# Attention inside a stream of projections: the last three value blocks of a head pair move into the next pair's first turn

## The reference, cut to what matters

```python
h = _rmsnorm(x, norm_g)
a_val, a_glu, z_a, q, k, v, z_b, g_logits = split(h @ w_in)
y_a = (_conv_module(a_val, a_glu, ...) * silu(z_a)) @ w_pw_a      # 31 taps along the tokens, per channel
attn = _neighbourhood_attention(q, k, v, rpb)                     # 16 heads of 64, window of 8 x 16 tokens
y_b = (attn * silu(z_b)) @ w_o_b
y = x + (sigmoid(g_a) * y_a + sigmoid(g_b) * y_b) @ w_out         # then a last rmsnorm
# attention of one query block j of 16 columns, against a band of 32 key columns:
s = einsum('bjqhd,bijkhd->bjqhik', qb, k_band) * scale + bias     # outside the window: -1e30
p = softmax(s)
o = einsum('bjqhik,bijkhd->bjqhd', p, v_band)
```

## Time and profile before

| | |
|---|---|
| median of three runs | 1718.92 us (1718.72 to 1720.77) |
| the profiled execution | 1718.98 us, span 1717.2 us |
| granted TensorE clock | 0.999 of full |
| PE busy | 1706.2 us, 99% |
| DVE, ACT, POOL busy | 1174.1, 470.5, 201.9 us |
| one unit of the loop | 145.02 us |
| the last unit and what follows it, 1198.93 to 1314.00 us | DVE 92.8 of 115.07 us, PE 113.4 |

### The profile page before, as it was taken

How to read it: one execution, slowest core, us unless ns; L and a number is a source line. 1 busy time by engine, 2 the same in 40 slices (tenths; PEclk the granted TensorE clock), 3 DMA queues, 4 the chain that set the end, 5 groups by cost and what they waited for, 6 DMA issues and landing times.

```text
span 1717.2 us, 25052 instructions
## 1 busy us (share of the span) xinstructions
PE 1706.2 (99%) x8644; PEld 1407.6 (82%) x8644; DVE 1174.1 (68%) x1875; ACT 470.5 (27%) x931; POOL 201.9 (12%) x251
## 2 busy tenths in 40 slices
PE   9999999999999999999999999999999999999998
PEld 7888888888888888888888888888887888888887
DVE  6549256896798589679678958967996755335332
ACT  5321123223122222222222222231234244003222
POOL 1110011001011001101101100010110064000001
PEclk9999999999999999999999999999999999999999
DMA  8761345445535444634552554454558775643223
GB/s 308 228 104 48 97 132 149 132 124 150 138 92 167 127 111 128 162 101 134 154 147 71 149 154 111 124 153 121 135 164 307 233 222 162 199 130 109 74 92 129
DMA packets 299204, 247.79 MB, mean 144 GB/s; under 512 B 117815, under 2 KB 252999, under 8 KB 298988
## 3 DMA queue, kind: packets, MB, share of 16 engines
q1 hardware_dynamic: 246666, 153.04, 32.5%
q10 hardware_dynamic: 48578, 79.97, 14.3%
q0 software_dynamic: 3872, 13.75, 3.1%
HBM read 158.78 MB, written 87.90 MB: 144 GB/s over the span
## 4 chain that ended last, share of the span: by engine, by line
PE 91%; DMA 4%; DVE 3%; issue 1%; SPq 1%; ACT 1%; POOL 0%; ACTq 0%; DVEq 0%; POOLq 0%
PE pg L1631 72%; PE pg L1649 11%; PE pS L1789 2%; PE pS L1808 2%; DMA x_d<-work 1%; PE pO L1808 1%; PE pO L1789 1%; DMA p_d<-work 1%; DVE xs L1188 1%; SPq L507 0%; DVE work L1385 0%; DMA work<-p_d 0%; DVE work L1387 0%; SPq L571 0%; PE pg L1676 0%
## 5 line engine op out<-in xcount | busy, mean ns | idle before, releaser
L1631 PE MATMUL pg<-xs,ws 128*128 128x512 f32 x5688 | 1304.2, 390 | 0.8 <-issue 0.6
L1631 PEld LDWEIGHTS pg<-xs,ws 128*128 128x128 f32 x5688 | 1064.2, 188 | 230.0 <-issue 8.2
L1302 DVE SCALAR_TENSOR_TENSOR work<-work 128x1551 f32<-128x1551 f32 x240 | 439.0, 1829 | 16.5 <-issue 11.8
L1649 PE MATMUL pg<-ws,xs 128*128 128x512 f32 x942 | 218.6, 389 | 0.7 <-DVE xs L1235 0.7
L1649 PEld LDWEIGHTS pg<-ws,xs 128*128 128x128 f32 x942 | 176.5, 188 | 37.9 <-issue 1.3
L733 POOL TENSOR_TENSOR work<-work 128x384 f32<-128x384 bf16 (+1 forms) x72 | 62.5, 868 | 964.2 <-DVE small L1375 952.1
L1026 ACT ACTIVATE work<-work,small 128x384 f32<-128x384 f32 (+1 forms) x192 | 109.4, 571 | 207.8 <-DVE small L1375 207.6
L1180 DVE TENSOR_TENSOR ws<-raw,ws 128x1024 fp32r<-128x1024 f32 x88 | 109.1, 1240 | 55.6 <-ACT ws L786 55.6
L786 ACT ACTIVATE ws<-raw 128x1024 fp32r<-128x1024 f32 x89 | 93.8, 1055 | 133.9 <-PE pg L1631 99.1
L1375 DVE CUSTOM_DVE_ANT_0 work<-pS,work 128x384 f32<-128x384 f32 (+1 forms) x128 | 58.0, 504 | 86.1 <-PE pS L1789 85.2
L1387 DVE STREAM_TRANSPOSE work<-work 128x384 f32<-128x384 f32 (+1 forms) x192 | 102.6, 534 | 6.6
(11 more groups left out here) (142 smaller groups left out, 1027.1 us busy)
## 6 DMA issues: line engine op xcount, KB each, us to landing
raw<-in_w_in SPq DMA_DIRECT2D x70, 512.0 KB, 3.8
p_d<-work SPq DMA_DIRECT2D x256, 96.0 KB, 2.1
work<-p_d ACTq DMA_DIRECT2D x63, 384.0 KB, 3.7
work<-v_d SPq DMA_DIRECT2D x128, 96.0 KB, 2.7
p_d<-work SPq DMA_DIRECT2D x128, 64.0 KB, 1.9
work<-p_d ACTq DMA_DIRECT2D x32, 256.0 KB, 3.0
v_d<-work ACTq DMA_DIRECT2D x24, 256.0 KB, 2.2
za_d<-work ACTq DMA_DIRECT2D x24, 256.0 KB, 2.1
```

Source lines behind the costliest of these rows:

```text
L1302: nc.vector.scalar_tensor_tensor(cv[:, 0:CLEN], u[:, k:k + CLEN], cur[:, k:k + 1], cv[:, 0:CLEN], ALU.mult, ALU.add).then_inc(tap_ok, 1)
L1631: last = nc.tensor.matmul(pg[b][:], wt(s, wpart)[:, k * P:(k + 1) * P], xs[:, k, xpart, chunk(n)], start=(j == 0 and wpart == 1), stop=(j ...
L1649: last = nc.tensor.matmul(pg[b][:], xs[:, k, xpart, t * P:(t + 1) * P], wt(s0 + k // 2, wpart)[:, chunk(k % 2)], start=(k == 0 and xpart = ...
```

## The change

The values of visit 3 of a pair (blocks 9, 10, 11) leave slot 41 and stand at slot 1 of the next unit, right ahead of that unit's first scores. In the code they are visit -1 of the next unit, with counts -3 to -1. `take_o` of these blocks moves on DVE from slot 42 to slot 2 of the next unit, behind the probabilities of block 1. In the last unit visit 3 stays at slot 30, and pair 6's last values come in at slot 1.

The values now need the pair's V until slot 1 of the next unit, so `load_v` moves on SP from the end of a unit to slot 4 of the next, right ahead of the first two blocks' stores. Its wait is taken by a separate nop, so that the 16 transfers are issued one after another behind it. The last third of `tb` is ready later, so the store of `tb` is split: two thirds at slot 33 (`tb_out`), the last third at slot 3 of the next unit (`tb_late`).

```diff
-VALUE_SLOTS = (11, 21, 31, 41)
+VALUE_SLOTS = (1, 11, 21, 31)
-FIRST_VALUES = (8, 15, 22, 29)
+FIRST_VALUES = (None, 8, 15, 22)
-LAST_VALUES = (8, 16, 23, 30)
+LAST_VALUES = (1, 8, 16, 23, 30)
@@ values_at
-    return table.index(slot) if slot in table else None
+    return table.index(slot) - 1 if slot in table else None
@@ load_v
-                after(sp, pv_done, used)
+                if not isinstance(i, int):
+                    sp.wait_ge(pv_done, used)
+                    sp.nop(nofuse=True)
+                else:
+                    after(sp, pv_done, used)
@@ SyncE, unit
                     c = scores_at(i, slot - 3)
+                    if c == 0 and not tiles is FIRST_UNIT:
+                        load_v(i, BLOCKS * i)
                     if c is not None:
                         for b in blocks_of(c)[0:2]:
                             store_probs(i, b)
...
-                if not last:
-                    load_v(i + 1, BLOCKS * i + BLOCKS)
@@ ScalarE, unit
-                    if values_at(i, slot - 2) == VISITS - 1 and not last:
-                        act.wait_ge(o_out, BLOCKS * i + BLOCKS)
-                        act.dma_start(row_of(tb_d, i), tb).then_inc(tb_out, 16)
+                    if values_at(i, slot - 2) == VISITS - 2 and not last:
+                        act.wait_ge(o_out, BLOCKS * i + 2 * BLOCKS // NCH)
+                        act.dma_start(row_of(tb_d, i)[:, 0:2 * CH], tb[:, 0:2 * CH]).then_inc(tb_out, 16)
+                    if slot == 3 and not first:
+                        act.wait_ge(o_out, BLOCKS * i)
+                        act.dma_start(row_of(tb_d, i - 1)[:, 2 * CH:TOK], tb[:, 2 * CH:TOK]).then_inc(tb_late, 16)
@@ VectorE, take_o
+                def take_o(count):
+                    b = count % BLOCKS
+                    dve.wait_ge(pv_done, BLOCKS * i + (count + 1))
+                    if count // VISIT < VISITS - 1:
+                        dve.wait_ge(qk_done, blk(i, blocks_of(count // VISIT + 1)[2], 1))
+                    if count >= 0:
+                        bz, _, oz = grp(i, s)
+                        dve.wait_ge(g_out[bz], oz)
@@ VectorE, evac of z_b
-                        after(dve, tb_out, 16 * i)
+                        after(dve, tb_late if n == NCH - 1 else tb_out, 16 * i)
@@ TensorE, values
-                def values(b):
+                def values(count):
+                    b = count % BLOCKS
-                    pe.wait_ge(p_in[b % VISIT], 16 * VISITS * i + 16 * (b // VISIT) + 16)
+                    pe.wait_ge(p_in[b % VISIT], 16 * VISITS * i + 16 * (count // VISIT) + 16)
```

More of the change, by code:

```diff
@@ L337, in build @@
         st_out = [sem(f"st_out{i}") for i in range(3)]
-        tb_out, c_out = sem("tb_out"), sem("c_out")
+        tb_out, tb_late, c_out = sem("tb_out"), sem("tb_late"), sem("c_out")
         cur_ok, curg_ok = sem("cur_ok"), sem("curg_ok")
@@ L578, in load_tb_early @@
                 sp.wait_ge(tb_out, 16 * (PAIRS - 1))
+                sp.wait_ge(tb_late, 16 * (PAIRS - 1))
                 piece_y(S_YB + 1)
@@ L1387, in probs @@
                     nc.vector.transpose(t, t).then_inc(tr_done, 1)
-                def take_o(b):
+                def take_o(count):
+                    b = count % BLOCKS
                     s, j = seg_of(b)
-                    dve.wait_ge(pv_done, BLOCKS * i + (b + 1))
-                    if b // VISIT < VISITS - 1:
-                        dve.wait_ge(qk_done, blk(i, blocks_of(b // VISIT + 1)[2], 1))
-                    bz, _, oz = grp(i, s)
-                    dve.wait_ge(g_out[bz], oz)
+                    dve.wait_ge(pv_done, BLOCKS * i + (count + 1))
[4 more added lines that the diff above has]
+                        dve.wait_ge(g_out[bz], oz)
                     z = tb[:, chunk(s)].rearrange("p (r j c) -> p j r c", j=4, c=QB)[:, j]
@@ L1781, in scores @@
                         after(pe, t_ok, 24 * i + 2 * b)
-                        after(pe, o_out, BLOCKS * i + max(b - VISIT, 0))
+                        after(pe, o_out, BLOCKS * i + (b - VISIT))
                     for qpart, kpart in ((q_lo, k_hi), (q_hi, k_lo), (q_hi, k_hi)):
@@ L1799, in values @@
                     if b % VISIT == 0:
-                        after(pe, t_ok, 24 * i + 2 * (b + VISIT))
-                        after(pe, o_out, BLOCKS * i + max(b - VISIT, 0))
+                        after(pe, t_ok, 24 * i + 2 * (count + VISIT))
+                        after(pe, o_out, BLOCKS * i + (count - VISIT))
                     for n, (c, a, z) in enumerate(REACH[s]):
@@ L1805, in values @@
                             rows = slice(HD * h, HD * h + HD)
-                            p = pt_of(i, b)[:, h].rearrange("p (a c q) -> p c a q", a=4, q=32)
+                            p = pt_of(None if count < 0 else i, b)[:, h].rearrange("p (a c q) -> p c a q", a=4, q=32)
                             o = o_of(b)[rows, :].rearrange("p (a q) -> p a q", a=4)
```

## The result

The changed kernel takes 1723.26 us (median of nine runs, 1721.08 to 1726.68), the kernel before 1719.42 beside it (nine runs, 1718.72 to 1721.39): ratio 1.0020, 95% interval 1.0010 to 1.0029. By the ratio it is slower by 3.4 us, between 1.7 and 5.0; the two medians are 3.8 us apart. That is just the 0.2% which the prediction took for what a measurement of this kernel can tell from no change. The forecast was 1721.2 in a range of 1717.5 to 1726.5. In two later jobs the medians stood 2.1 and 2.3 us apart, and the interval of the second (0.9999 to 1.0017) does not exclude no change.

The account below looks back on a forecast made before the run. The prediction took TensorE, at its own pace without idle time in the loop, as the bound. Interruptions saved (-1.54), loop (0) and last unit (+3.8) gave +2.3 us on 1718.98, hence 1721.2 us, range 1717.5 to 1726.5.

Parts of the forecast that it names:

- The gain of 1.54: TensorE, pairs 0 to 6: one interruption of a matmul run fewer per pair, 0.22 us each, 1.54 us gained.
- SP and the third block: V's issues delay stores; DVE starts the third block 14.9 us (loop) or 14.6 (last unit) after t, TensorE's slot 1.
- the rival without late stores: V's issues as short as its data, stores not held up: 0.3 us lost in the last unit, 1717.7; chance 0.08.
- DVE's own arrival: Loop: with three take_o ahead, DVE reaches the third block at 12.75 us, then stands still until 14.9.
- No pause in the loop: Loop, slot 8: group 2 released at 22.15 us, TensorE asks at 22.3; fits by 0.15 us, costs nothing.
- The first rival: Loop units pause too, once the third block starts after 15.1 us; 1724.6 with stores 0.6 us later; chance 0.33.
- The last unit: New TensorE pause of 3.2 us at slot 6, waiting for group 1; DVE's chain stays 5.6 us late.
- the term of 3.8: Last unit: its end moves 5.6 us, 1.8 of it moved values, so 3.8 us lost (ends 3.4 and 6.5).
- The clock rival: Granted clock falls to 1.2 GHz during the last unit's 3.2 us pause: 1.6 us more, 1722.8; chance 0.04.
- Against: 1.00 throughout: Argument against the clock falling: the granted clock read 1.00 in both profiled windows of the kernel before.
- The sum: Whole kernel: -1.54 + 0 + 3.8 = +2.3 us, hence 1721.2 us.
- 1719.8 to 1722.3: Whole-kernel time if the last unit loses and the loop does not: the main forecast, chance 0.52.

Follow-up runs that it names:

- v_split: Changed kernel with V's 16 transfers in units 1 to 7 issued half by SyncE, half by GpSimd; ratio 0.9997 to the kernel before.
- v_pool: Changed kernel with V of units 1 to 7 issued by GpSimd, ahead of its third bias kind; ratio 1.0053 to the kernel before.
- v_dose: Changed kernel with two more 96 KB transfers issued by SyncE behind V's 16 in each loop unit; ratio 1.0039 to the kernel before.
- v_alone: Kernel before with only V's transfers moved ahead of the first stores, values and take_o left in place; ratio 1.0045 to the kernel before.
- after_again: The changed kernel run a second time, nothing edited; ratio 1.0014 to the kernel before.
- after_third: The changed kernel run a third time, nothing edited; ratio 1.0008 to the kernel before.
- v_pool_last: Changed kernel with V of the last unit alone issued by GpSimd, ahead of its third bias kind; ratio 0.9998 to the kernel before.
- v_pool3_last: Changed kernel with V of the last unit alone issued by GpSimd, behind its third bias kind; ratio 0.9999 to the kernel before.

## Why the prediction was right, step by step

- **The gain of 1.54.** Right: 0.23 for each interruption, 1.41 in all after a pause of 0.34 in unit 1 that belongs to the step on the loop.
- **SP and the third block.** The sizes were near: V at t + 2.1, stores from t + 10.2, third block at 14.2 to 14.6 for 14.9 and 13.7 to 14.2 for 14.6, which is at and below the lower end of 14.2 that I gave. The 9.19 us taken for V's issues in the loop were 8.0. The cause was half the story. I made the issues the price, and the rival without late stores assumed that short issues would free them; v_split has issues out of the way and the block at 13.6.
- **DVE's own arrival.** Wrong without consequence: 12.75 was 13.48 (v_pool and all that don't hold it), because I left out that the first scores come 1.8 us later as well. DVE's idle stretch in the loop is 0.7 to 1.0 and not 2.
- **No pause in the loop.** Right for units 2 to 6 in every profile that has V's 16 on SP ahead of the stores and no dose, 30 units. Unit 1 pauses 0.1 to 0.55 in the same six profiles, its third block starting at 14.9 to 15.4, and the bound was 14.82. The first rival's mechanism is real (v_dose, v_alone); it misses by 0.2 us in the other units.
- **The last unit.** The place and the mechanism were right, the term of 3.8 was too small: 4.66, 4.59 and 6.64 in three profiles. In the first, DVE's chain does what the prediction said and a little less: block 8's scores are 4.8 later on DVE for the 5.6 forecast. The term was too small because it took P's return as unchanged: block 8's P takes 3.96 and 4.52 us instead of 3.04 and 4.17, 1.3 more, and TensorE waits 0.4 more for P at slot 30. 4.8 + 1.3 + 0.4 are the 6.5. So 3.8 came near because an overestimate and an omission partly cancel. In after_again it is 6.3 (with the slow spell), 0.0 and 0.2, in after_third 6.5, 1.0 and the second spell's 1.5, less 0.4 at slot 30, where TensorE doesn't wait.
- **The clock rival.** Its size came out, 1.6 us a spell, by luck: it was worked out as half the pause's own length, and the spells are equally long behind pauses of 1.73 and 3.05 us. Its chance of 0.04 was too small: it fell in two of three profiles of the changed kernel. The step that failed here is the argument "Against: 1.00 throughout", which came from rows without such a pause.
- **The sum.** +2.3 forecast; 2.4 in the profiled execution, 3.8, 2.1 and 2.3 by the medians. The 2.4 is partly luck: the stretch grew by 3.25, and 0.9 came back ahead of it and behind it, in work that the change doesn't touch. The median of the first comparison, 1723.26, lies in the range and outside the 1719.8 to 1722.3 that had the highest chance.

Open stays what part of the first comparison's 3.8 is the clock's, since an execution without a profile shows no clock by stretch, and why the store of block 8's P takes 3.0 us once and 4.0 another time.

## What to carry to other kernels

A piece of work moved from the end of a loop's turn into the next turn gains a little per turn, and its last instance lands in the unit behind the loop, where the room may be smaller: price that unit by itself. Before putting a burst of transfers ahead of small urgent ones, ask how long its data takes and not only its issues, and if it must stand there, fetch first only what is needed first. Of the nine places in these profiles where TensorE newly stood still for over 2 us, six had a spell of the lower clock behind them, so such a pause should be given 1.6 us more as a likely price. No version here beats the kernel before: v_split, v_pool_last and v_pool3_last equal it, with intervals that reach 0.1% to either side.

## What the runs showed of the hardware

- The granted clock fell to 1.2 GHz behind pauses of TensorE of 2.41, 2.62, 2.70, 2.77 and 3.05 us at slot 6, of 2.44 at slot 8 and of 1.73 at slot 23, and did not behind 2.15 and 2.21 at slot 6 and 2.44 at slot 23 in other executions. A spell cost about 1.6 us where it fell.
- Transfers of 96 KB in rows of 512 bytes land one per 0.6 us, issued by one engine (changed kernel) or by two (v_split). A store issued beside them takes 4.9 us to land instead of 2.0.
- A tensor_scalar of 0.35 us and a scalar_tensor_tensor of 1.82 us on VectorE took up to 3.3 us beside GpSimd's additions. In the kernel before the same two meet and the longest tensor_scalar is 1.2 us, so a shift of either engine by a few microseconds may open or close this.
